# Expert passes: the pass with one expert of 128 rows moves from eighth to tenth, and the weight loads of the last five passes follow

## The chip, the core and the metric

One NeuronCore of one Trainium2 chip runs the whole program. The metric is the device time in microseconds of one execution. Before the change the median of three runs is 1499.13 us (1495.96 to 1499.97). TensorE (PE) does the matrix products, VectorE (DVE) and ScalarE (ACT) the work between them, GpSimd (POOL) issues indexed transfers, and SyncE (SP) issues the weight loads and writes the result.

## The reference, cut to what matters

The program is a two-layer encoder trunk over 512 tokens of width 1024, in float32. Each layer has an attention mixer, which the change leaves alone, and then a grouped top-2 mixture of 16 SwiGLU experts with hidden width 512:

```python
def expert_block(args):
    xb, e = args
    return (jax.nn.silu(xb @ w1[e]) * (xb @ w3[e])) @ w2[e]
...
return jnp.zeros((T, D), h.dtype).at[tok_sorted].add(ys[dest] * g_sorted[:, None].astype(h.dtype))
```

Every token goes to two experts. Each expert has three weight matrices, w1 and w3 (1024 x 512) and w2 (512 x 1024), of 2048 KB each: 48 matrices and 96 MB for each layer.

## The kernel before, in words

**Passes and places.** The experts of a layer are worked off in 11 passes of 128 token rows (`PASSES`). A place is a position in the order in which experts are worked off; `EXPERT_RANK` (line 59) says which expert stands at which place: two experts are fixed (places 0 and 1), the others are sorted on the chip by how many tokens they got, and a place takes the expert of a given rank. `TILES` (line 60) splits each pass into tiles `(place, first row, rows)` of 32, 64 or 128 rows, so that up to four tiles of up to three experts share a pass. Tokens beyond the rows given to a rank go to extra passes behind, under a condition.

**One pass on TensorE** (lines 2405 to 2438, in the order of issue): the first up product (w1, `up_tiles` with m = 0, L2387), the second up product (w3, m = 1, L2387), the transposes of the next pass's tokens (L2353), the down product of the pass before (w2, `down_tiles`, L2398), the transposes of this pass's hidden rows (L2373). So the down product of pass p is issued in pass p + 1. The last pass is different: the down product of pass 9 stands between its two up products, and its own comes last. Ahead of an up product TensorE waits until the weights of all places in that pass have landed (`loaded(j, m)`), ahead of a down product likewise (L2394). When a product is done it adds to a semaphore: `h1_r`, `h3_r` (once for each pass) and `y_r` (twice for each pass).

**Weight slots.** There are eight slots of 2048 KB: six in `ring`, slot 6 is the tile `hT`, slot 7 is `reg_a`. `MOE_LOADS` (line 86) is the list of all 48 loads of a layer as `(place, matrix, slot)`, matrix 0, 1, 2 being w1, w3, w2. A slot is used again for the next load in the list that names it.

**The order of the loads.** It is written out by hand in SyncE's program (lines 706 to 805): a wait for the product that frees the slot, then the load, in the order of `MOE_LOADS`. All of them go to one queue. SyncE is in order, so a load whose slot is free still stands behind the waits of those before it. After the 48 loads come the first weights of the next layer's input projection (`load_z`, layer 0 only), then the read-back of the expert outputs from memory (`load_outputs`, L808).

**Beside them.** GpSimd gathers the token rows of each pass by an indexed transfer from `xn_d` (L916) and scatters the outputs to `ys_d` (L924), each 512 KB, on another queue of the same transfer engines. ScalarE computes the sigmoid and moves transposed data out of PSUM, VectorE multiplies (L1797, L1802) and scales the outputs (L1811).

The lines that the change touches and the prediction's steps use: `EXPERT_RANK` and `TILES` (59 to 70), `MOE_LOADS` (86 to 93), SyncE's loads from place 10 on (757 to 805), TensorE's waits in `loaded` (2376 to 2379) and the loop over passes (2405 to 2441). Passes are numbered from 0 here: the eighth is pass 7, the tenth pass 9.

Of the kernel before, what the change touches and what calls it, by code (L numbers as in the profile page):

```python
# [55 lines left out]

PASSES = 11
STATIC = (11, 12)
EXPERT_RANK = (14, 15, 9, 0, 4, 5, 10, 1, 8, 13, 2, 6, 7, 11, 12, 3)
TILES = (((0, 0, 32), (0, 32, 32), (0, 64, 32), (1, 96, 32)),  # L60
         ((1, 0, 64), (2, 64, 64)),
         ((3, 0, 128),),
# [1 line left out]
         ((5, 0, 64), (6, 64, 64)),  # L64
         ((7, 0, 128),),
         ((8, 0, 32), (8, 32, 32), (8, 64, 32), (9, 96, 32)),
         ((10, 0, 128),),
         ((11, 0, 32), (11, 32, 32), (11, 64, 32), (12, 96, 32)),
         ((12, 0, 32), (12, 32, 32), (13, 64, 32), (14, 96, 32)),
         ((15, 0, 128),))  # L70
FIRST_ROWS = sum(n for j, at, n in TILES[0] if j == 0)

# [1 line left out]
def rows_by_rank():  # L74

    first, rows = [None] * E, [0] * E
    for p, tiles in enumerate(TILES):
        for j, at, n in tiles:
            r = EXPERT_RANK[j]
            first[r] = p * P + at if first[r] is None else first[r]  # L80
# [13 lines left out]
MOE_SLOT = {(j, m): s for j, m, s in MOE_LOADS}  # L94

TR_N1, TR_QK, TR_LAT, TR_KR, TR_N2, TR_X0 = 0, 8, 13, 18, 21, 29
# [88 lines left out]
def trunk(nc, x_in, c_in, w_ada, b_ada, norm1, w_in, q_norm_a, k_norm_a, q_a_norm, kv_norm, w_q_b,  # L185
# [29 lines left out]
    with ExitStack() as ctx:  # L215
# [3 lines left out]
        def sem(name):  # L219
            return ctx.enter_context(nc.semaphore(name))  # L220
# [159 lines left out]
        def slot(s, a, n):  # L380
            if s == R:
                return hT[:, :, :].rearrange("p c n -> p (c n)")[:, 0:a * n].rearrange("p (a n) -> p a n", a=a)
            if s == R + 1:
                return reg_a[:, 0:a * n].rearrange("p (a n) -> p a n", a=a)
            return ring[:, s, 0:a * n].rearrange("p (a n) -> p a n", a=a)
# [125 lines left out]
        h1_r, h3_r = sem("h1_ready"), sem("h3_ready")  # L511
        sge_s = sem("h1_sigmoid")
        u_s_s = sem("expert_hidden")
        y_r, y_e = sem("expert_out_ready"), sem("expert_out_read")
# [33 lines left out]
        def wait(eng, s, value):  # L548

            eng.wait_ge(s, value)  # L550
            eng.sem_inc(ticks, 1)
# [23 lines left out]
        def _(sp):  # L575
# [27 lines left out]
            def load_z(layer, i):  # L603
                at, n = Z_ITEMS[i]
                load(i, (NC, n), in_v[layer, :, :, at:at + n])
# [4 lines left out]
            for l in range(DEPTH):  # L610
# [63 lines left out]
                def load_w1(j, e):  # L674
                    s = MOE_SLOT[j, 0]
                    sp.dma_start(slot(s, NC, F), w1_v[l * E + e]).then_inc(w_rdy[s], 16)

                def load_w3(j, e):
                    s = MOE_SLOT[j, 1]
                    sp.dma_start(slot(s, NC, F), w3_v[l * E + e]).then_inc(w_rdy[s], 16)  # L680

                def load_w2(j, e):
                    s = MOE_SLOT[j, 2]
                    sp.dma_start(slot(s, 4, D), w2_v[l * E + e]).then_inc(w_rdy[s], 16)
# [14 lines left out]
                def expert_at(j):  # L699

                    r = EXPERT_RANK[j]
                    return sp.value_load(order_i[0:1, r:r + 1], min_val=0, max_val=E - 1)
                rank = [None] * E
# [53 lines left out]
                rank[10] = expert_at(10)  # L757
                wait(sp, h3_r, l * PASSES + 6)
                load_w1(10, rank[10])
                wait(sp, y_r, (l * PASSES + 5) * 2)  # L760
                load_w3(10, rank[10])
                wait(sp, y_r, (l * PASSES + 5) * 2)
                load_w2(8, rank[8])
                wait(sp, h1_r, l * PASSES + 7)
                load_w2(9, rank[9])
                rank[11] = expert_at(11)
                wait(sp, h1_r, l * PASSES + 7)
                load_w1(11, rank[11])
                rank[12] = expert_at(12)
                wait(sp, h3_r, l * PASSES + 7)  # L770
                load_w1(12, rank[12])
                wait(sp, h3_r, l * PASSES + 7)
                load_w3(11, rank[11])
                wait(sp, y_r, (l * PASSES + 6) * 2)
                load_w3(12, rank[12])
                wait(sp, h1_r, l * PASSES + 8)
                load_w2(10, rank[10])
                rank[13] = expert_at(13)
                wait(sp, h3_r, l * PASSES + 8)
                load_w1(13, rank[13])  # L780
                rank[14] = expert_at(14)
                wait(sp, y_r, (l * PASSES + 7) * 2)
                load_w1(14, rank[14])
                wait(sp, y_r, (l * PASSES + 7) * 2)
                load_w3(13, rank[13])
                wait(sp, h1_r, l * PASSES + 9)
                load_w3(14, rank[14])
                wait(sp, h3_r, l * PASSES + 9)
                load_w2(11, rank[11])
                wait(sp, y_r, (l * PASSES + 8) * 2)  # L790
                load_w2(12, rank[12])
                rank[15] = expert_at(15)
                wait(sp, h1_r, l * PASSES + 10)
                load_w1(15, rank[15])
                wait(sp, h1_r, l * PASSES + 10)
                load_w2(13, rank[13])
                wait(sp, h1_r, l * PASSES + 10)
                load_w2(14, rank[14])
                wait(sp, h3_r, l * PASSES + 10)
                load_w3(15, rank[15])  # L800
                wait(sp, h3_r, l * PASSES + 10)
                load_w2(15, rank[15])
                if l < DEPTH - 1:
                    wait(sp, h3_r, l * PASSES + 10)
                    load_z(l + 1, 0)

                def load_outputs(t, done):
# [1679 lines left out]
```

## Time and profile before

| what | value |
|---|---|
| median of the runs | 1499.13 us (1495.96 to 1499.97) |
| the profiled execution's own time | 1496.24 us |
| its span, first to last instruction | 1494.5 us |
| PE busy | 1417.9 us (95%) |
| DVE, ACT, POOL busy | 666.3, 397.4, 73.5 us |
| moved by transfers | 346.77 MB, mean 232 GB/s |
| weight loads of the experts | 72 into `ring`, 12 into `reg_a`, 12 into `hT`, 2048 KB each |
| granted TensorE clock, mean | 0.987 |

The busy share of a span is a mean over stages. The expert stages lie at about 490 to 750 us (layer 0) and 1220 to 1475 us (layer 1). An idle time in a timeline row stands in brackets with what ended it. For a transfer the profile gives the instruction that issues it, and the time from there to its landing.

### The profile page before, as it was taken

What the parts mean: (1) busy time and instruction counts of PE and PEld (TensorE: products, weight loads), DVE (VectorE), ACT (ScalarE), POOL (GpSimd) and SP (SyncE); (2) the same over time, 40 slices, a digit from 0 to 9 for tenths busy, and PEclk for the clock granted to TensorE, in tenths of its full rate; (3) what the DMA queues carried; (4) which work ended last, traced back from release to release, by engine and by line L of the source; (5) the groups of instructions that cost most, each with busy time, mean ns of one, the idle gap of its engine ahead of it and who ended that gap; (6) DMA issues with size and microseconds to landing.
All of it is one profiled execution on the core that took longest, in us unless ns stands there. A gap on an engine that the chain in (4) does not pass through costs nothing.

```text
span 1494.5 us, 19619 instructions
## 1 busy us (share of the span) xinstructions
PE 1417.9 (95%) x7656; PEld 790.2 (53%) x7657; DVE 666.3 (45%) x1368; ACT 397.4 (27%) x934; POOL 73.5 (5%) x104
## 2 busy tenths in 40 slices
PE   4989999999998899999999999999999969999997
PEld 2655666777744343343346675677775423343333
DVE  6588676575734311111166877553332260111115
ACT  3227555100012222122041575430001122111212
POOL 1000000000000100100010000000000000011000
PEclk9999999999999899999999999999999979999999
DMA  9963026234273799999976603310306268999994
GB/s 324 383 213 103 18 97 226 85 90 136 94 286 141 294 417 395 422 422 423 368 277 269 173 1 114 114 43 1 113 0 267 94 260 355 412 401 422 425 413 189
DMA packets 113359, 346.77 MB, mean 232 GB/s; under 512 B 26582, under 2 KB 57414, under 8 KB 99888
## 3 DMA queue, kind: packets, MB, share of 16 engines
q1 hardware_dynamic: 87616, 305.68, 53.5%
q0 software_dynamic: 9008, 31.41, 5.6%
q10 hardware_dynamic: 16640, 8.39, 1.9%
q8 instruction: 62, 1.02, 0.3%
q14 instruction: 33, 0.27, 0.1%
HBM read 331.55 MB, written 21.00 MB: 236 GB/s over the span
## 4 chain that ended last, share of the span: by engine, by line
PE 86%; DMA 6%; DVE 4%; ACT 2%; issue 1%; DVEq 1%; SPq 0%; POOLq 0%; ACTq 0%
PE bank L2387 18%; PE bank L2086 13%; PE bank L2398 9%; PE bank L2293 7%; PE bank L2133 7%; PE bank L2016 6%; PE bank L2172 4%; DMA ring<-in_w 3%; PE bank L2228 2%; PE bank L2192 2%; PE bank L2242 2%; PE bank L2201 2%; PE bank L1976 2%; PE bank L1947 2%; DMA ring<-in_w_ada 1%; PE bank L2069 1%
## 5 line engine op out<-in xcount | busy, mean ns | idle before, releaser
L2387 PE MATMUL bank<-ring,reg_b 128*32 128x512 f32 (+2 forms) x1312 | 268.3, 603 | 2.1 <-ACT reg_b L1197 2.1
L2387 PEld LDWEIGHTS bank<-ring,reg_b 128*32 128x32 f32 (+2 forms) x1312 | 86.2, 125 | 139.2 <-issue 136.4
L2398 PE MATMUL bank<-ring,reg_b 128*32 128x512 f32 (+2 forms) x768 | 141.5, 594 | 6.4 <-DMA ring<-in_w 5.0
L2016 PE MATMUL bank<-ring,hT 128*128 128x256 f32 (+3 forms) x448 | 128.6, 448 | 1.2 <-ACT reg_b L1044 1.2
L2293 PE MATMUL bank<-ring,reg_b 128*128 128x512 f32 x256 | 113.0, 596 | 0.0
L2133 PE MATMUL bank<-reg_a,ring 128*128 128x512 f32 x256 | 112.7, 593 | 0.0
L1197 ACT ACTIVATE reg_b<-bank,cur 128x128 f32<-128x128 f32 x176 | 64.0, 470 | 164.7 <-PE bank L2353 164.7
L2016 PEld LDWEIGHTS bank<-ring,hT 128*128 128x128 f32 x448 | 84.8, 190 | 43.1 <-issue 16.5
L1811 DVE TENSOR_TENSOR reg_d<-bank,reg_c 128x512 f32<-128x512 f32 x44 | 30.3, 691 | 135.3 <-PE bank L2398 135.2
L2398 PEld LDWEIGHTS bank<-ring,reg_b 128*32 128x32 f32 (+2 forms) x768 | 47.6, 123 | 78.3 <-issue 75.8
L2086 PE MATMUL bank<-hT,ring 128*128 128x256 f32 x384 | 88.1, 379 | 0.0
L1482 DVE TENSOR_REDUCE nmax<-bank 128x1 f32<-128x512 f32 x128 | 79.5, 684 | 16.1 <-PE bank L2233 12.2
L1797 DVE TENSOR_TENSOR reg_b<-bank,reg_b 128x512 f32<-128x512 f32 x22 | 15.2, 692 | 158.1 <-ACT reg_b L1204 158.1
L2387 PE MATMUL bank<-hT,reg_b 128*32 128x512 f32 (+2 forms) x288 | 84.6, 593 | 0.0
L2086 PEld LDWEIGHTS bank<-hT,ring 128*128 128x128 f32 x384 | 72.8, 190 | 15.8 <-issue 6.7
L2293 PEld LDWEIGHTS bank<-ring,reg_b 128*128 128x128 f32 x256 | 47.7, 190 | 56.3 <-issue 56.3
L2133 PEld LDWEIGHTS bank<-reg_a,ring 128*128 128x128 f32 x256 | 48.5, 190 | 54.6 <-issue 53.9
L1802 DVE TENSOR_TENSOR reg_b<-bank,reg_b 128x512 f32<-128x512 f32 x22 | 15.2, 692 | 123.6 <-PE bank L2387 123.6
L2086 PE MATMUL bank<-ring 128*128 128x256 f32 x256 | 57.9, 379 | 0.0
L2387 PE MATMUL bank<-reg_a,reg_b 128*32 128x512 f32 (+2 forms) x192 | 56.5, 594 | 0.0
L2086 PEld LDWEIGHTS bank<-ring 128*128 128x128 f32 x256 | 48.5, 190 | 6.5
L1204 ACT ACTIVATE reg_b<-bank 128x512 f32<-128x512 f32 x22 | 13.1, 597 | 142.7 <-PE bank L2387 142.7
(352 smaller groups left out, 1951.4 us busy)
## 6 DMA issues: line engine op xcount, KB each, us to landing
ring<-in_w SPq DMA_DIRECT2D x72, 2048.0 KB, 15.4
ring<-in_w_ada SPq DMA_DIRECT2D x16, 2048.0 KB, 11.8
reg_a<-in_w SPq DMA_DIRECT2D x12, 2048.0 KB, 12.8
hT<-in_w SPq DMA_DIRECT2D x12, 2048.0 KB, 15.5
ring<-in_w_in SPq DMA_DIRECT2D x9, 2048.0 KB, 8.0
ring<-in_w_ada SPq DMA_DIRECT2D x16, 512.0 KB, 9.6
vb<-in_w_ada ACTq DMA_DIRECT2D x16, 512.0 KB, 4.0
ring<-in_w_o SPq DMA_DIRECT2D x4, 2048.0 KB, 9.1
```

What stands on the lines that cost most here:

```text
L1197: ins = A(xsT[:, b, cc, :], bank[(p0 + k) % 2][:, c * P:(c + 1) * P], ACT.Identity, scale=scale2(cc), bias=shift2(cc))
L1482: v.tensor_reduce(nmax[:, i:i + 1], bank[4 + i][:, :], X, ALU.max, negate=True).then_inc(mx_s, 1)
L1811: TT(ysb[:, p, cols], bank[6 + n][:, :], g2_row[:, cols], ALU.mult).then_inc(y_e, 1)
L1947: ins = pe.transpose(bank[g % 2][0:rows, t * P:(t + 1) * P], src, ident)
L1976: ins = pe.matmul(bank[z_bank(t)][:, 0:n], hT[:, c, t * P:(t + 1) * P], slot(0, NC, n)[:, c, :], start=c == 0, stop=c == NC - 1)
L2016: ins = pe.matmul(bank[z_bank(k)][:, 0:n], hT[:, c, t * P:(t + 1) * P], w[:, c, :], start=c == 0, stop=c == NC - 1)
L2086: ins = pe.matmul(bank[bk][:, half * 256:(half + 1) * 256], w[:, c, :], tokens[:, c, :], start=c == 0, stop=c == 3)
L2133: ins = pe.matmul(branch_bank(j, q)[:, :], w[:, c, (j % 4) * P:(j % 4 + 1) * P], oT[:, c + 4 * q, :], start=c == 0, stop=c == 3)
L2172: ins = pe.transpose(bank[prob_bank(u)][:, kc * P:(kc + 1) * P], prob[(k - 1) % 2][i][:, kc * P:(kc + 1) * P], ident)
L2293: ins = pe.matmul(wo_bank(k)[:, :], mT[:, c, t * P:(t + 1) * P], w[:, c, :], start=c == 0, stop=c == NC - 1)
L2387: ins = pe.matmul(bank[bk][at:at + n, :], xsT[:, p % 2, c, at:at + n], slot(MOE_SLOT[j, m], NC, F)[:, c, :], start=c == 0, stop=c == NC - 1)
L2398: ins = pe.matmul(bank[6 + h][at:at + n, :], uT[:, c, at:at + n], slot(MOE_SLOT[j, 2], 4, D)[:, c, h * 512:(h + 1) * 512], start=c == 0, s ...
```

## The change

Places 10 to 14 take other ranks: the rank 2 (128 rows) goes from place 10 to place 14, the ranks 6, 7, 11 and 12 each move one place forward. The tiles of passes 7 to 9 follow: pass 7 now has three tiles of place 10 and one of place 11, pass 8 two tiles of place 11, one of place 12 and one of place 13, pass 9 one tile of 128 rows of place 14. Pass 10 is as before. The last 20 of the 48 loads stand in a new order, with slots and waits to match, and the next layer's first `load_z` waits for another product.

```diff
--- before.py
+++ after.py
@@ -56,7 +56,7 @@
 
 PASSES = 11
 STATIC = (11, 12)
-EXPERT_RANK = (14, 15, 9, 0, 4, 5, 10, 1, 8, 13, 2, 6, 7, 11, 12, 3)
+EXPERT_RANK = (14, 15, 9, 0, 4, 5, 10, 1, 8, 13, 6, 7, 11, 12, 2, 3)
 TILES = (((0, 0, 32), (0, 32, 32), (0, 64, 32), (1, 96, 32)),
          ((1, 0, 64), (2, 64, 64)),
          ((3, 0, 128),),
@@ -64,9 +64,9 @@
          ((5, 0, 64), (6, 64, 64)),
          ((7, 0, 128),),
          ((8, 0, 32), (8, 32, 32), (8, 64, 32), (9, 96, 32)),
-         ((10, 0, 128),),
-         ((11, 0, 32), (11, 32, 32), (11, 64, 32), (12, 96, 32)),
-         ((12, 0, 32), (12, 32, 32), (13, 64, 32), (14, 96, 32)),
+         ((10, 0, 32), (10, 32, 32), (10, 64, 32), (11, 96, 32)),
+         ((11, 0, 32), (11, 32, 32), (12, 64, 32), (13, 96, 32)),
+         ((14, 0, 128),),
          ((15, 0, 128),))
 FIRST_ROWS = sum(n for j, at, n in TILES[0] if j == 0)
 
@@ -87,10 +87,10 @@
              (2, 0, 7), (2, 1, 6), (3, 0, 3), (3, 1, 4), (2, 2, 1), (4, 0, 7),
              (5, 0, 5), (4, 1, 6), (5, 1, 0), (3, 2, 3), (6, 0, 4), (6, 1, 2),
              (4, 2, 1), (5, 2, 7), (7, 0, 6), (7, 1, 3), (6, 2, 5), (8, 0, 4),
-             (9, 0, 0), (8, 1, 2), (9, 1, 1), (7, 2, 6), (10, 0, 3), (10, 1, 7),
-             (8, 2, 5), (9, 2, 4), (11, 0, 0), (12, 0, 2), (11, 1, 1), (12, 1, 6),
-             (10, 2, 3), (13, 0, 7), (14, 0, 5), (13, 1, 4), (14, 1, 0), (11, 2, 1),
-             (12, 2, 3), (15, 0, 2), (13, 2, 7), (14, 2, 5), (15, 1, 6), (15, 2, 4))
+             (9, 0, 0), (8, 1, 2), (9, 1, 1), (7, 2, 6), (10, 0, 3), (11, 0, 5),
+             (10, 1, 7), (11, 1, 0), (8, 2, 4), (9, 2, 1), (12, 0, 2), (13, 0, 6),
+             (12, 1, 3), (13, 1, 7), (10, 2, 1), (11, 2, 4), (14, 0, 5), (14, 1, 2),
+             (12, 2, 6), (13, 2, 0), (15, 0, 3), (14, 2, 7), (15, 1, 1), (15, 2, 5))
 MOE_SLOT = {(j, m): s for j, m, s in MOE_LOADS}
 
 TR_N1, TR_QK, TR_LAT, TR_KR, TR_N2, TR_X0 = 0, 8, 13, 18, 21, 29
@@ -757,51 +757,51 @@
                 rank[10] = expert_at(10)
                 wait(sp, h3_r, l * PASSES + 6)
                 load_w1(10, rank[10])
+                rank[11] = expert_at(11)
+                wait(sp, y_r, (l * PASSES + 5) * 2)
+                load_w1(11, rank[11])
                 wait(sp, y_r, (l * PASSES + 5) * 2)
                 load_w3(10, rank[10])
-                wait(sp, y_r, (l * PASSES + 5) * 2)
+                wait(sp, h1_r, l * PASSES + 7)
+                load_w3(11, rank[11])
+                wait(sp, h1_r, l * PASSES + 7)
                 load_w2(8, rank[8])
-                wait(sp, h1_r, l * PASSES + 7)
+                wait(sp, h3_r, l * PASSES + 7)
                 load_w2(9, rank[9])
-                rank[11] = expert_at(11)
-                wait(sp, h1_r, l * PASSES + 7)
-                load_w1(11, rank[11])
                 rank[12] = expert_at(12)
                 wait(sp, h3_r, l * PASSES + 7)
                 load_w1(12, rank[12])
-                wait(sp, h3_r, l * PASSES + 7)
-                load_w3(11, rank[11])
+                rank[13] = expert_at(13)
                 wait(sp, y_r, (l * PASSES + 6) * 2)
+                load_w1(13, rank[13])
+                wait(sp, h1_r, l * PASSES + 8)
                 load_w3(12, rank[12])
-                wait(sp, h1_r, l * PASSES + 8)
+                wait(sp, h3_r, l * PASSES + 8)
+                load_w3(13, rank[13])
+                wait(sp, y_r, (l * PASSES + 7) * 2)
                 load_w2(10, rank[10])
-                rank[13] = expert_at(13)
-                wait(sp, h3_r, l * PASSES + 8)
-                load_w1(13, rank[13])
+                wait(sp, y_r, (l * PASSES + 7) * 2)
+                load_w2(11, rank[11])
                 rank[14] = expert_at(14)
-                wait(sp, y_r, (l * PASSES + 7) * 2)
+                wait(sp, h1_r, l * PASSES + 9)
                 load_w1(14, rank[14])
-                wait(sp, y_r, (l * PASSES + 7) * 2)
-                load_w3(13, rank[13])
                 wait(sp, h1_r, l * PASSES + 9)
                 load_w3(14, rank[14])
+                wait(sp, h1_r, l * PASSES + 9)
+                load_w2(12, rank[12])
                 wait(sp, h3_r, l * PASSES + 9)
-                load_w2(11, rank[11])
+                load_w2(13, rank[13])
+                rank[15] = expert_at(15)
+                wait(sp, h3_r, l * PASSES + 9)
+                load_w1(15, rank[15])
+                wait(sp, h3_r, l * PASSES + 9)
+                load_w2(14, rank[14])
                 wait(sp, y_r, (l * PASSES + 8) * 2)
-                load_w2(12, rank[12])
-                rank[15] = expert_at(15)
+                load_w3(15, rank[15])
                 wait(sp, h1_r, l * PASSES + 10)
-                load_w1(15, rank[15])
-                wait(sp, h1_r, l * PASSES + 10)
-                load_w2(13, rank[13])
-                wait(sp, h1_r, l * PASSES + 10)
-                load_w2(14, rank[14])
-                wait(sp, h3_r, l * PASSES + 10)
-                load_w3(15, rank[15])
-                wait(sp, h3_r, l * PASSES + 10)
                 load_w2(15, rank[15])
                 if l < DEPTH - 1:
-                    wait(sp, h3_r, l * PASSES + 10)
+                    wait(sp, y_r, (l * PASSES + 9) * 2)
                     load_z(l + 1, 0)
 
                 def load_outputs(t, done):
```

## Rows read from the trace of the kernel before

**Rows 1.** The page, section 4: shares by engine of the chain that ended last.
```profile
PE 86%; DMA 6%; DVE 4%; ACT 2%; issue 1%; DVEq 1%; SPq 0%; POOLq 0%; ACTq 0%
```

**Rows 2.** TensorE's waits, whole span: who <- whom: us in total, times, longest us.
```profile
PE bank L2398 <- DMA ring<-in_w: 5.0, 4, 1.8
```

**Rows 3.** Timeline of PE, layer 0: start us, us, what [idle before <- releaser].
```profile
707.80 7.07 PE L2398 MATMUL bank<-ring,reg_b 128*32 128x512 f32 x64 [1.01 <-DMA ring<-in_w]
...
724.12 0.62 PE L2398 MATMUL bank<-ring,reg_b 128*32 128x512 f32 x2 [1.78 <-DMA ring<-in_w]
```

**Rows 4.** Timeline of PE, layer 1, the same places.
```profile
1434.82 1.49 PE L2398 MATMUL bank<-ring,reg_b 128*32 128x512 f32 x12 [1.04 <-DMA ring<-in_w]
...
1450.53 0.62 PE L2398 MATMUL bank<-ring,reg_b 128*32 128x512 f32 x2 [1.18 <-DMA ring<-in_w]
```

**Rows 5.** Table by stretch: length, busy by engine, clock, DMA share, GB/s.
```profile
600.00:700.00 100.00, 100.00 (x604) 39.31 (x600) 12.23 (x18) 17.61 (x42) 9.07 (x9) 1.00 1.01 422
```

**Rows 6.** Timeline of SP, layer 0: start us and length of three issues.
```profile
647.09 0.33 SPq L680 DMA_DIRECT2D hT<-in_w  x1
...
661.34 0.34 SPq L676 DMA_DIRECT2D reg_a<-in_w  x1
...
669.77 0.33 SPq L680 DMA_DIRECT2D ring<-in_w  x1
```

**Rows 7.** Transfers issued by them, in turn: KB, us from issue to landing.
```profile
hT<-in_w SPq DMA_DIRECT2D x1, 2048.0 KB, 23.3
...
reg_a<-in_w SPq DMA_DIRECT2D x1, 2048.0 KB, 19.8
...
ring<-in_w SPq DMA_DIRECT2D x1, 2048.0 KB, 22.2
```

**Rows 8.** The chain of waits in order of time, layer 0: start us, us, what.
```profile
661.98 7.00 PE bank L2398 x64
...
669.57 13.87 PE bank L2387 x128
...
684.53 6.87 PE bank L2398 x16
```

**Rows 9.** Transfers, layer 0, issued at 639.23 us (first row) and 699.11 (second).
```profile
ring<-in_w SPq DMA_DIRECT2D x1, 2048.0 KB, 20.2
...
ring<-in_w SPq DMA_DIRECT2D x1, 2048.0 KB, 13.5
```

**Rows 10.** Timeline of SP, layer 1: two issues.
```profile
1388.33 0.33 SPq L676 DMA_DIRECT2D reg_a<-in_w  x1
...
1396.75 0.33 SPq L680 DMA_DIRECT2D ring<-in_w  x1
```

**Rows 11.** The transfers issued by these two, in turn.
```profile
reg_a<-in_w SPq DMA_DIRECT2D x1, 2048.0 KB, 19.2
...
ring<-in_w SPq DMA_DIRECT2D x1, 2048.0 KB, 21.9
```

**Rows 12.** The chain of waits, layer 1.
```profile
1396.55 13.87 PE bank L2387 x128
...
1411.51 6.87 PE bank L2398 x16
```

**Rows 13.** Timeline of PE, the end of layer 0.
```profile
749.39 1.12 PE L1928 MATMUL bank<-reg_d 128*128 128x512 f32 x2 [1.87 <-DVE reg_d L1811]
```

**Rows 14.** Timeline of PE: two longer waits, and the first up product of layer 1.
```profile
112.40 1.09 PE L1947 MATMUL bank<-cst,reg_b 128*128 128x128 f32 x8 [3.06 <-DVE reg_b L1329]
...
1207.45 0.31 PE L2329 MATMUL bank<-reg_f,cst 128*128 128x64 bf16 x4 [4.11 <-DVE reg_f L1654]
...
1220.56 15.53 PE L2387 MATMUL bank<-ring,reg_b 128*32 128x512 f32 x128 [0.39 <-ACT reg_b L1197]
```

**Rows 15.** Table by stretch, for the clock (the column before the last two).
```profile
100.00:125.00 25.00, 20.38 (x106) 12.85 (x105) 21.11 (x49) 12.02 (x32) 2.98 (x7) 1.00 0.78 211
...
1207.00:1220.00 13.00, 3.94 (x46) 3.48 (x46) 10.48 (x48) 1.00 (x3) 1.08 (x1) 0.50 0.42 136
```

## The prediction

> **What bounds the kernel now.** I read the chain of waits first: PE carries 86% of it and transfers 6% [rows 1]. The change touches only the last part of the two expert stages, so next I read TensorE's waits over the whole execution. Four waits for a weight transfer, all at the down product (L2398), come to 5.0 us [rows 2]. The timeline puts them in the last passes: 1.01 us before the down product of pass 8 and 1.78 us before that of pass 9 in layer 0 [rows 3], 1.04 and 1.18 us at the same places in layer 1 [rows 4]. The stretch table says what they hang on: from 600 to 700 us PE is busy for 100.00 of 100.00 us, the DMA engines stand at a share of 1.01 and move 422 GB/s [rows 5]. So two things are full at once, and the transfers have a backlog: the load issued at 661.34 us takes 19.8 us to land [rows 6, 7], though 2048 KB at 422 GB/s are 5.0 us of work. It stands in line behind some three others.
>
> That gives the model for what follows. All weights go out on SP's queue in the order of the SyncE program, and a weight lands when everything ahead of it has been moved. An earlier issue doesn't bring a landing forward; only an earlier position does.
>
> **The change part by part.**
> *TensorE's work.* Passes 7 to 10 hold the same tiles in another order, and the rows of capacity by rank stay the same, so no expert gets more or fewer rows. Passes of four tiles take 13.87 us for both up products, as the one shown here [rows 8]; the down products of four tiles and of one take 7.00 and 6.87 us [rows 8]. Cost: 0.
>
> *SyncE's work.* 20 weight loads before and after, 20 issues of 0.3 to 0.4 us [rows 6], hidden behind a backlog of about 20 us. If that cover were gone, a late issue would cost at most one place in line, 5 us. The next layer's first z load goes out 21st in line as before, at the down product of pass 8. Cost: 0.
>
> *What each pass asks of the line.* Count loads from w1 of place 10, the first in the changed part, as number 1. Before, the up products of pass 8 need places 11 and 12, and the last of their four weights is number 8. After, they need 11, 12 and 13: w1 of 13 is number 8, needed when the pass starts, and w3 of 13 is number 10, needed at its half. The down product of pass 7 needed number 9 (w2 of 10); after, it needs w2 of 10 and of 11, and the latter is number 12. In return the down product of pass 8 needs number 16 (before: 15), and that of pass 9 number 18 as before, and PE comes to both later by what it has lost.
>
> Now the clock, in layer 0. Number 8 lands at 647.09 + 23.3 = 670.39 us, number 10 at 661.34 + 19.8 = 681.14, number 12 at 669.77 + 22.2 = 691.97 [rows 6, 7]: 10.8 us between each two, 5.4 for one place. I take these landings over to the new order position by position: up to number 12 each position is released by the same event as before, all weights are 2048 KB, and the gathers and scatters beside them keep their times until PE first stalls.
> - Pass 8 starts at 669.57 [rows 8] and waits for number 8: 0.8 us. Its first half (half of 13.87, 6.9) ends at 677.3.
> - The second half waits for number 10 until 681.1: 3.8 us. It ends at 688.1, the token transposes (684.53 - 669.57 - 13.87 = 1.1) at 689.2.
> - The down product of pass 7 waits for number 12 until 692.0: 2.8 us. Before, it began at 684.53 [rows 8]. From here PE is 691.97 - 684.53 = 7.4 us late.
> - Pass 9 would start at about 699.3 and needs numbers 13 and 14; at 5.4 us a place they land at 697.4 and 702.8, the second for its half at 706.2. No wait.
> - The down product of pass 8 would start at 707.80 - 1.01 + 7.4 = 714.2 and needs number 16, which lands at 699.11 + 13.5 = 712.6 [rows 9]: a margin of 1.6 us. The 1.01 us there is gone. Number 18 landed when the wait before pass 9's down product ended, 724.1 [rows 3]; it is now wanted at 724.12 - 1.78 - 1.01 + 7.4 = 728.7. The 1.78 us is gone too.
> - Sum for layer 0: 7.4 - 1.0 - 1.8 = **+4.6 us**.
>
> Layer 1, the same way: number 10 lands at 1388.33 + 19.2 = 1407.53 [rows 10, 11], where the half of pass 8 was due at 1396.55 + 6.9 = 1403.5 [rows 12]: 4.1 us for pass 8. Number 12 lands at 1396.75 + 21.9 = 1418.65 [rows 10, 11], and the down product of pass 7 began at 1411.51 [rows 12]: PE is 7.1 us late, 3.1 of it here. Less 1.04 and 1.18: **+4.9 us**.
>
> What could be given back behind it: at the end of layer 0 PE waits 1.87 us for VectorE's output step [rows 13], which follows outputs read back beside z's load. PE will be later and that load not, so up to 1.87 us of it may go; in layer 1 there is no such wait. I take 0 (PE's own last product sets this end nearly as late) and leave the other end to the range. Bounds of the main term: a whole place in line more or less at number 12 would be +5.4 or -5.4 us in each layer. The row nearest is its own, and over the two layers it stands 7.4 and 7.1 us behind the product that will need it, so I use 1 us each way.
>
> Earlier passes aren't hit: the nearest is the down product of pass 6, which starts at 661.98 [rows 8] and needs number 6, at 639.23 + 20.2 = 659.4 [rows 9]. A margin of 2.5 us.
>
> The sum is +9.5 us on the profiled execution's own 1496.24 us (span 1494.5): 1505.7. The median shown is 1499.13 us, 2.9 above that execution: 1508.6. I forecast between the two, **1507.5 us**.
>
> A rule of the Trainium skill (DMA: Bandwidth & Descriptors, "Queues, rings and completion order") speaks against landings pinned to their position: completion isn't in issue order for one issuing engine. By it number 12 could come a place sooner, 5.4 us, and the sum would be near nothing, about 1498 us. The loads read here land in the order of their issue [rows 6, 7, 9 to 11], so the trace does not bear it out.
>
> **The rivals.**
> *The clock falls in the new waits.* Waits of 3.8 us in the middle of dense work are longer than any that the expert passes have now. For it: behind a wait of 4.11 us in layer 1 the granted clock stood at 0.50 (1.2 GHz) from 1207 to 1220 us [rows 14, 15]. Against: a wait of 3.06 us at 112 us lies in a stretch at 1.00 [rows 14, 15], and at the place of that fall PE had little work for longer than the one wait. Price: that up product took 15.53 us [rows 14] where 13.87 is usual, so 1.7 us for each time. The wait for number 12 hides what follows number 10; one or two falls in each layer that do show are 3.4 to 6.8 us: about 1512. The Trainium skill (TensorE: Matmul & The Clock Gate, "Why this matters for your kernels") says that idle gaps between bursts of matmuls put the clock back to its lower level; by that rule this rival would be the forecast.
>
> *Arrivals keep pace in part.* If releases and not bytes spaced the landings, the earlier places would land earlier. For it: before the change many loads wait for a slot. Against: the share of 1.01 all through [rows 5]. If number 12 landed 4.7 us sooner, nothing is lost or won: about 1498.
>
> *Faster: the waits vanish and nothing comes for them.* One mechanism: a line that isn't full at pass 8, so that number 12 lands before 684.5, 7.4 us earlier than its row. It turns faster from the point where number 12 lands before 687.3. In the end the 5.0 us of [rows 2] are gone: 1499.13 - 5.0 = 1494.1. Against it stands the same share of 1.01.
>
> *Worse: a margin breaks.* The 1.6 us at the down product of pass 8 or the 2.5 us at that of pass 6 fails, and one more place is waited for, 5.4 less the margin, 3 to 4 us in each layer: about 1515.
>
> **How the numbers follow.** Forecast 0.72 (own range 1503.5 to 1511), clock 0.12, in part 0.08, faster 0.04, worse 0.04. 0.3% is 4.5 us, about what a measurement of this kernel can tell from no change: 1494.6 to 1503.6. Faster is the one rival, 0.04; within are "in part" and the low end of the forecast, 0.12; slower 0.84. The range 1502.5 to 1513.5 leaves out faster, "in part", "worse" and the end of the clock's.
>
> **What will show it.** In the changed profile: waits for a weight transfer at L2387 in pass 8, 0.8 and then 3.8 us in layer 0 (4.1 together in layer 1), then 2.8 and 3.1 us at the down product of pass 7; no wait for a transfer at those of passes 8 and 9; numbers 8, 10 and 12 landing within 1 us of the rows here; pass 9 starting 7 us later than before, the last down product 4 to 5 us. If number 10 lands by 677, the model of the line is wrong. If the clock of the stretch behind the waits is under 1.00, the first rival holds.

## The result, and the profile after

The changed kernel takes 1511.1 us (median of 4, 1509.65 to 1513.19) against 1499.55 us for the kernel before, measured beside it (median of 4): ratio 1.0076, 95% interval 1.0063 to 1.0089. Its profiled execution took 1510.24 us (span 1508.5), 14.0 more than that of before. "Late" below is later than before; places in line are counted from w1 of place 10 as number 1, as in the prediction.

TensorE's waits of the kernel after, whole span; these three stand where [rows 2] stood:

```profile
PE bank L2387 <- DMA reg_a<-in_w: 6.7, 2, 3.5
...
PE bank L2398 <- DMA ring<-in_w: 3.5, 2, 1.8
...
PE bank L2387 <- DMA hT<-in_w: 1.7, 2, 1.4
```

5.0 us of waits for weights went and 11.9 us came, partly at another product: L2387 is the up product. The timeline of PE after, layer 0, then layer 1, gives the places; it answers to [rows 3, 4]:

```profile
674.29 0.63 PE L2387 MATMUL bank<-ring,reg_b 128*32 128x512 f32 x3 [0.32 <-DMA hT<-in_w]
...
684.59 0.63 PE L2387 MATMUL bank<-ring,reg_b 128*32 128x512 f32 x3 [3.23 <-DMA reg_a<-in_w]
...
696.22 1.07 PE L2398 MATMUL bank<-ring,reg_b 128*32 128x512 f32 x8 [1.76 <-DMA ring<-in_w]
...
1406.20 0.63 PE L2387 MATMUL bank<-ring,reg_b 128*32 128x512 f32 x3 [1.42 <-DMA hT<-in_w]
...
1416.76 1.07 PE L2387 MATMUL bank<-ring,reg_b 128*32 128x512 f32 x3 [3.48 <-DMA reg_a<-in_w]
...
1428.10 1.49 PE L2398 MATMUL bank<-ring,reg_b 128*32 128x512 f32 x11 [1.71 <-DMA ring<-in_w]
```

They are the start of pass 8 (number 8), its half (number 10) and the down product of pass 7 (number 12). The chain of waits after, layer 0, shows that behind them no weight is waited for: the products of passes 8 to 10 follow each other.

```profile
666.38 7.05 PE bank L2398 x64
...
696.22 7.08 PE bank L2398 x64
...
703.88 13.73 PE bank L2387 x32
...
718.50 7.00 PE bank L2398 x64
...
732.96 6.87 PE bank L2398 x16
```

The loads: SP's timeline (start, length), layer 0, for numbers 8, 10 and 12, and then how long each of the three took to land. They answer to [rows 6, 7]:

```profile
651.22 0.35 SPq L676 DMA_DIRECT2D hT<-in_w  x1
...
665.48 0.33 SPq L680 DMA_DIRECT2D reg_a<-in_w  x1
...
673.57 0.94 SPq L684 DMA_DIRECT2D ring<-in_w  x2
```
```profile
hT<-in_w SPq DMA_DIRECT2D x1, 2048.0 KB, 22.9
...
reg_a<-in_w SPq DMA_DIRECT2D x1, 2048.0 KB, 19.0
...
ring<-in_w SPq DMA_DIRECT2D x1, 2048.0 KB, 22.0
```

Number 12 is the second of the two issues in the third row of SP's timeline, at 674.12. The three land at 674.12, 684.48 and 696.12 us. Pass 5's up product begins at 606.76 (602.71 before), so that is 67.4, 77.7 and 89.4 us behind it; in the trace of before the same positions landed 67.7, 78.4 and 89.3 us behind it. The line is the same in layer 0; what PE asks of it has changed. In layer 1 (pass 5 at 1337.58, before 1329.69) the landings come 68.5, 79.0 and 90.4 us behind, against 67.3, 77.8 and 89.0: 1.2 to 1.4 us later. No run here says why; the other profiles of the changed kernel spread as much there (number 10 ends its wait 76.8 us behind pass 5's start in again, 79.2 in after).

The stretch table after, its columns as in [rows 5]:

```profile
600.00:674.00 74.00, 73.97 (x500) 27.61 (x492) 9.54 (x14) 14.10 (x36) 6.06 (x6) 1.00 1.01 422
...
684.00:694.00 10.00, 9.41 (x70) 3.54 (x71) 0.58 (x1) 0.00 (x0) 0.00 (x0) 0.83 1.04 420
694.00:704.00 10.00, 8.23 (x74) 3.35 (x73) 1.45 (x3) 2.98 (x9) 0.00 (x0) 1.00 0.99 418
...
1416.00:1426.00 10.00, 9.24 (x70) 3.16 (x71) 0.63 (x1) 0.01 (x1) 0.00 (x0) 0.83 1.04 423
```

The transfers run at 1.01 and 422 GB/s as before. New is 0.83 in the clock column (1.00 is 2.4 GHz), just behind the wait for number 10: the second half of pass 8 took 8.77 us instead of 7.07 in layer 0, 8.54 in layer 1. It cost nothing, since number 12 landed later still.

**Where the 14 us are.** I take the distance from the start of pass 5's up product to the start of the last down product as the length of a stage. Before: 137.67 and 137.11 us (layer 0, layer 1); after: 142.06 and 143.13, so +4.4 and +6.0. At the end of layer 0 the wait of [rows 13] is 1.18 us instead of 1.87, 0.7 less. The change need not have done this: in a second profile of the kernel before (experiment before2) it is 1.19 us too. The remaining 4.05 us were there before pass 5 of layer 0 began, ahead of anything that the change touches. The table shows them at about 112 and 515 us:

```profile
112.00:120.00 8.00, 6.89 (x32) 3.23 (x32) 5.21 (x15) 2.05 (x4) 1.31 (x4) 0.57 1.01 328
...
514.00:520.00 6.00, 5.33 (x20) 1.80 (x20) 0.00 (x0) 1.54 (x5) 0.41 (x1) 0.72 0.89 371
```

The clock fell there, and did not in the first trace of before: at 112 us it has 1.00 [rows 15], and at 515 us

```profile
514.00:520.00 6.00, 6.00 (x30) 2.01 (x28) 0.00 (x0) 0.12 (x1) 0.00 (x0) 1.00 0.54 227
```

The second profile of before has both falls too (its table shows 0.76 from 513 to 520 us), at 112 us

```profile
112.00:120.00 8.00, 6.86 (x32) 3.21 (x32) 5.15 (x15) 2.17 (x4) 1.23 (x4) 0.57 1.00 327
```

Its pass 5 begins at 606.65 us, and its span is 1499.3: so this part is chance between executions. Against that span the change costs 9.2 us.

### The profile page after: what moved, and what is told of

It reads as the page before. It is cut to its first block, busy times and chain, and to the rows that moved or that the text cites. A ratio compares the mean times of both kernels' runs of the same rounds, so it can differ in the third digit from the quotient of the medians.

```text
span 1508.5 us, 19619 instructions
## 1 busy us (share of the span) xinstructions
PE 1425.6 (95%) x7656; PEld 794.4 (53%) x7657; DVE 666.2 (44%) x1368; ACT 397.0 (26%) x934; POOL 73.5 (5%) x104
## 4 chain that ended last, share of the span: by engine, by line
PE 86%; DMA 6%; DVE 4%; ACT 2%; issue 1%; DVEq 1%; SPq 0%; POOLq 0%; ACTq 0%
PE bank L2387 18%; PE bank L2086 13%; PE bank L2398 10%; PE bank L2293 7%; PE bank L2133 7%; PE bank L2016 6%; PE bank L2172 4%; DMA ring<-in_w 3%; PE bank L2228 2%; PE bank L2242 2%; PE bank L2201 2%; PE bank L1976 2%; PE bank L2192 2%; PE bank L1947 2%; DMA ring<-in_w_ada 2%; PE bank L2069 1%
## 5 line engine op out<-in xcount | busy, mean ns | idle before, releaser
L2387 PE MATMUL bank<-ring,reg_b 128*32 128x512 f32 (+2 forms) x1344 | 300.7, 610 | 10.6 <-DMA reg_a<-in_w 6.7
L2387 PEld LDWEIGHTS bank<-ring,reg_b 128*32 128x32 f32 (+2 forms) x1344 | 100.3, 130 | 165.4 <-issue 160.9
L2398 PE MATMUL bank<-ring,reg_b 128*32 128x512 f32 (+2 forms) x736 | 127.4, 594 | 4.8 <-DMA ring<-in_w 3.5
L2398 PEld LDWEIGHTS bank<-ring,reg_b 128*32 128x32 f32 (+2 forms) x736 | 40.9, 120 | 69.4 <-issue 62.8
L2387 PE MATMUL bank<-reg_a,reg_b 128*32 128x512 f32 (+1 forms) x256 | 61.4, 614 | 0.0
L2387 PE MATMUL bank<-hT,reg_b 128*32 128x512 f32 (+2 forms) x192 | 56.3, 593 | 0.0
```

The costliest lines, as they stand in the source:

```text
L2387: ins = pe.matmul(bank[bk][at:at + n, :], xsT[:, p % 2, c, at:at + n], slot(MOE_SLOT[j, m], NC, F)[:, c, :], start=c == 0, stop=c == NC - 1)
L2398: ins = pe.matmul(bank[6 + h][at:at + n, :], uT[:, c, at:at + n], slot(MOE_SLOT[j, 2], 4, D)[:, c, h * 512:(h + 1) * 512], start=c == 0, s ...
```

## The experiments

The theory: landings follow from the position in line, and three of the moved passes now ask for positions earlier than before. The rivals: a late issue, waits spread over the whole line, and the clock.

**1. again**, the changed kernel once more.

> The changed kernel once more, unchanged. Theory A (the line of loads: a weight lands when everything ahead of it has been moved, and the change puts the weights of pass 8 and the down product of pass 7 further back): waits for transfers in pass 8 and before the down product of pass 7 come back within 0.5 us (3.2 and 1.8 us in layer 0, 1.4, 3.5 and 1.7 in layer 1), the expert stages together are 9 to 11 us longer than before. The first profile of the changed kernel was 4 us late before it reached the changed part, where the granted clock had fallen twice more than in the profile of before. If that is chance from one execution to the next, it is absent or of another size here and the median is 9.5 to 12 us above before; if the change causes it, it is here again at the same two places.

1508.49 us, 8.8 above before, ratio 1.006 [1.0046, 1.0074]. Of the three places two wait, those of number 10 and number 12; number 8 comes just in time in both layers. The waits did not come back within the 0.5 us expected (3.63 us for 1.76 at the second), and the time is a little under the expected 9.5. The falls at 112 and 515 us are absent. And here the clock held at the wait for number 10 and fell at the next, PE's timeline:

```profile
680.06 0.63 PE L2387 MATMUL bank<-ring,reg_b 128*32 128x512 f32 x3 [2.67 <-DMA reg_a<-in_w]
...
691.86 8.74 PE L2398 MATMUL bank<-ring,reg_b 128*32 128x512 f32 x64 [3.63 <-DMA ring<-in_w]
```

and the stretch just behind it (0.51 in the clock column is 1.2 GHz, with PE busy for all of it):

```profile
691.90:695.30 3.40, 3.40 (x20) 0.90 (x24) 0.00 (x0) 0.00 (x0) 0.00 (x0) 0.51 0.97 414
```

The down product took 8.74 us instead of 7.08, in layer 1 8.77. So the fall can come at either wait. At the first, it eats into the second wait (1.76 instead of 3.63), and at the second it shows. The stages are nearly the same, 142.9 in each layer against 142.1 and 143.1, because the wait for number 12 also ended sooner here, by 0.8 us in layer 0 and 1.9 in layer 1 against pass 5's start.

**2. late10**: issue number 10 later, in the same place in line.

```diff
-                wait(sp, h3_r, l * PASSES + 8)
+                wait(sp, y_r, (l * PASSES + 6) * 2 + 1)
                 load_w3(13, rank[13])
```

> The changed kernel, with one wait moved: load number 10 (w3 of place 13) is issued after the first half of the down product of pass 6, some 3.6 us later than now; its place in the line stays. Theory A: its landing does not move (within 0.5 us, relative to the start of pass 5), the waits in pass 8 stay at 3 to 3.5 us, and the time is that of the changed kernel within 1 us. Rival (a landing follows from its own issue, 19 us later): it lands 3.6 us later, the wait at the half of pass 8 grows to about 7 us, and the time by 1 to 3 us in each layer.

SP's timeline, of again, then of late10, there with PE's row for the half of pass 8:

```profile
661.89 0.33 SPq L680 DMA_DIRECT2D reg_a<-in_w  x1
```
```profile
668.12 0.33 SPq L680 DMA_DIRECT2D reg_a<-in_w  x1
...
681.50 1.07 PE L2387 MATMUL bank<-ring,reg_b 128*32 128x512 f32 x3 [2.54 <-DMA reg_a<-in_w]
```

The issue moved 4.7 us (58.7 to 63.4 us behind pass 5's start). The half of pass 8, which that load releases, begins 76.75 us behind it against 76.88 in again. In layer 1 it begins 1.2 us later than in again (78.05 for 76.84), more than the 0.5 expected; but there the line was late before the moved load: number 7 landed 62.6 us behind pass 5's start (again 61.7). The trace has no landing of number 10 itself, so the end of PE's wait stands for it. The time is 1509.04 us, ratio 1.0058 [1.0044, 1.0072], the same. The moment of issue did not count here, where the line was full.

**3. cut11**: of w2 of place 10 only the first of its four quarters is loaded, so number 11 is 512 KB and everything behind it should land about 4 us sooner.

```diff
-                    sp.dma_start(slot(s, 4, D), w2_v[...]).then_inc(w_rdy[s], 16)
+                    n = 1 if j == 10 else 4
+                    sp.dma_start(slot(s, 4, D)[:, 0:n, :], w2_v[...][:, 0:n, :]).then_inc(w_rdy[s], 16)
```

> The changed kernel, but of w2 of place 10 (load number 11) only a quarter is loaded, so one product uses old data; the issues and waits are the same. Theory A: number 10 lands as before, number 12 lands 3.8 us sooner, the wait before the down product of pass 7 (1.8 and 1.7 us) is gone, and the time is 3.5 us below the changed kernel, not more, since the fall of the clock behind the wait for number 10 (1.7 us in each layer) is no longer hidden by the wait for number 12. Without that fall being on the path it would be 5.7 to 6 us. Rival (releases set the landings): the landings and the time stay.

1500.5 us, ratio 1.0007 [0.9995, 1.0019]. Of the waits for weights this is left (its lines are one higher):

```profile
PE bank L2388 <- DMA reg_a<-in_w: 5.7, 2, 3.2
```

The wait for number 12 is gone in both layers, the one for number 10 has stayed. Number 11 lands 79.9 us behind pass 5's start in layer 0 (again 83.4), and number 14, of full size, 94.9 (98.4): bytes ahead in line set the landing. It brought 8.0 us against again, where 3.5 was expected. In again the second wait is 3.6 us in each layer with a visible fall of 1.7 behind it. The waits went in both layers; the fall went only in layer 1, where none came. In layer 0 it came behind the first wait and now shows (8.77 us). Stages 139.86 and 137.38.

**4. swap**: the kernel before, with only w3 of place 12 moved back from number 8 to number 10. Order of passes, tiles and ranks stay.

```diff
-             ... (11, 1, 1), (12, 1, 6), (10, 2, 3), (13, 0, 7), (14, 0, 5), ...
+             ... (11, 1, 1), (10, 2, 3), (13, 0, 7), (12, 1, 6), (14, 0, 5), ...
-                wait(sp, y_r, (l * PASSES + 6) * 2)
-                load_w3(12, rank[12])
                 ...
                 load_w1(13, rank[13])
+                wait(sp, h3_r, l * PASSES + 8)
+                load_w3(12, rank[12])
```

> The kernel before with its passes as they were, and one load two places later in the line: w3 of place 12 (number 8) becomes number 10, behind w2 of place 10 and w1 of place 13. Theory A: it lands at about 681 us in layer 0, 4.6 us after the half of pass 8 (4.0 in layer 1); the two old waits before the down products of passes 8 and 9 (2.8 and 2.2 us) vanish in exchange. With the clock as it is: +1.8 us in each layer, +3.6 in all over before. If the clock falls in that wait, nothing hides it here: 1.7 us more in each layer, +7 in all. If the loss of the change came from the order of the passes and not from the places in the line, this kernel costs nothing.

1504.66 us, ratio 1.0036 [1.0022, 1.0049]. PE's timeline, layer 0 and 1:

```profile
682.21 0.63 PE L2387 MATMUL bank<-ring,reg_b 128*32 128x512 f32 x3 [3.63 <-DMA hT<-in_w]
...
1414.47 1.07 PE L2387 MATMUL bank<-ring,reg_b 128*32 128x512 f32 x3 [6.17 <-DMA hT<-in_w]
```

The half of pass 8 now needs number 10, and waits as it does in the changed kernel, though no pass was moved; the waits of [rows 3, 4] are gone. The 6.17 us of layer 1 are 2.2 more than expected; why number 10 landed so late there, 79.9 us behind pass 5's start, stays open. The halves behind took 8.77 and 8.43 us, with nothing later to hide them. With both falls 7 us over before were expected: the stages of this profile are 7.3 over the mean of before's (140.26 and 142.47), the median is 5.0 over.

**5. before2**: the kernel before, unchanged, with a profile of its own.

> The kernel before once more, for a second profile of it. Theory A: waits of 1 to 2 us before the down products of passes 8 and 9 in both layers, 4.5 to 6 us in all, no wait for a transfer in pass 8, and the distance from the start of pass 5 to the last down product within 1 us of that of the first profile (137.7 and 137.1 us). The clock falls of the changed kernel behind its waits for weights are absent; falls elsewhere (near 112 us, and in the first passes of layer 1) may come or not, as chance has it, in both kernels.

Ratio 0.9996 [0.9983, 1.0009]. Its waits stand at the same places as [rows 3, 4], 1.60 and 1.81 us in layer 0, 1.08 and 1.78 in layer 1 (the profile puts the 1.08 down to ScalarE); its stages are 138.29 and 137.75 us. So a stage varies by 0.6 us between executions, and the mean of three profiles of the changed kernel (142.6) stands 4.9 us above the mean of two of before (137.7) in each layer: 9.8 us in all.

**6. m_2121**: the one-expert pass from place 8 goes to place 9, not 10, so passes 7 to 10 bring 2, 1, 2, 1 new experts (before 1, 2, 2, 1; after 2, 2, 1, 1). Loads follow.

```diff
-         ((10, 0, 128),),
-         ((11, 0, 32), (11, 32, 32), (11, 64, 32), (12, 96, 32)),
-         ((12, 0, 32), (12, 32, 32), (13, 64, 32), (14, 96, 32)),
+         ((10, 0, 32), (10, 32, 32), (10, 64, 32), (11, 96, 32)),
+         ((12, 0, 128),),
+         ((13, 0, 32), (13, 32, 32), (13, 64, 32), (14, 96, 32)),
          ((15, 0, 128),))
```

> A fourth order: passes 7 to 10 bring 2, 1, 2, 1 new experts, so the pass with one expert of 128 rows is ninth, half the way of the change. Theory A: the last of the four up weights of pass 9 is number 14 in the line; it lands at about 702.5 us in layer 0 and 1429.6 in layer 1, 3.7 us after the half of pass 9 in both, and the two old waits vanish in exchange (2.8 and 2.2 us): +2.5 us over before if the clock stays up, +6 if it falls behind this wait in both layers, since no second wait hides it. Nothing is waited for in pass 8.

1503.32 us, ratio 1.0025 [1.0014, 1.0037]. One place is left that waits, the half of pass 9:

```profile
705.60 8.35 PE L2387 MATMUL bank<-ring,reg_b 128*32 128x512 f32 x64 [3.77 <-DMA ring<-in_w]
...
1434.08 8.77 PE L2387 MATMUL bank<-ring,reg_b 128*32 128x512 f32 x64 [2.37 <-DMA ring<-in_w]
```

The clock fell behind both. This half asks for number 14, where before it asked for number 13. With both falls 6 us over before were expected; 3.5 were measured, as number 14 landed 100.2 us behind pass 5's start in layer 0 but 98.7 in layer 1. So the pass need not go all the way to place 10 to cost: pass 6 brings two new experts as well, and what counts is how many weights PE has asked for by then.

**7. fill and fill2**: the changed kernel with products on constants put in just before the two waits, 5 calls (fill) or 2 (fill2) at each. Nothing reads their result.

```diff
+                def fill(n):
+                    for _ in range(n):
+                        pe.matmul(bank[3][:, :], ident, cst[:, 0:512], start=True, stop=True)
 ...
+                        if p == 8 and m == 1:
+                            fill(2)
 ...
+                        if p == 8:
+                            fill(2)
```

> The changed kernel with ten more products in each layer, which fill its two long waits and feed nothing: five of 128x512 (2.1 us) ahead of the half of pass 8 and five ahead of the down product of pass 7. If the clock falls because TensorE is idle there, it stays at 1.00 in these stretches and the time is 1 to 3.5 us below the changed kernel, whose falls cost 1.7 us each when they come behind the second wait. If the clock has nothing to do with these waits, the time is the same or up to 2 us above, where a wait is shorter than its filling.

> The changed kernel with four more products in each layer that feed nothing, two at each long wait (1.8 us each time; the five of the last such kernel took 4.46 us and outlasted the waits by 1.3 to 2.2 us). They fit into waits of 2.5 us and more. If idle time is what lowers the clock, it stays at 1.00 in passes 8 and 9, and the time is up to 3.4 us below that of the changed kernel in this call (1.7 us for each fall that no later wait hides). If the fall is not on the path, the times are the same.

In fill the 5 calls took 4.56 us,

```profile
679.19 4.56 PE L2393 MATMUL bank<-cst 128*128 128x512 f32 x10
```

outlasted the landings by 1.2 to 2.2 us and so replaced the waits: 1510.56 us, ratio 1.0076 [1.0063, 1.0088]. So it can't give the price of a fall, though the clock stayed at 1.00 in these passes. In fill2 they took 1.9 to 2.0 us and left waits of 1.1 to 1.9:

```profile
681.58 0.63 PE L2387 MATMUL bank<-ring,reg_b 128*32 128x512 f32 x3 [1.11 <-DMA reg_a<-in_w]
...
693.39 7.07 PE L2402 MATMUL bank<-ring,reg_b 128*32 128x512 f32 x64 [1.93 <-DMA ring<-in_w]
```

The table for the ten microseconds behind the first of them, fill2 and then again2:

```profile
682.00:692.00 10.00, 9.46 (x76) 3.77 (x68) 0.69 (x1) 2.66 (x8) 0.00 (x0) 1.00 1.04 419
```
```profile
682.00:692.00 10.00, 9.84 (x72) 3.79 (x72) 0.69 (x1) 0.39 (x2) 0.00 (x0) 0.83 1.05 422
```

**8. again2**, the changed kernel beside fill2 on the same chip.

> The changed kernel, to stand beside the filled one on the same chip: 9 to 11 us above before, waits of some 3 us at the half of pass 8 and 2 to 4 us before the down product of pass 7, the clock down for 3.4 us at one of them in each layer.

1508.36 us, ratio 1.0058 [1.0043, 1.0073]; fill2 1507.89, 1.0055 [1.004, 1.007]. In again2 the clock fell at the first wait in both layers (3.22 us, half product 8.76), and the second wait took it up (1.61). Expected were 9 to 11 us over before; 8.6 were measured. So a clock held at 1.00 in fill2 brought 0.5 us, which can't be told from nothing: where the second wait hides the fall, keeping the clock up is worth nothing that shows.

**9. c_1212**: passes 7 to 10 bring 1, 2, 1, 2 new experts. No two passes with two of them stand together.

```diff
          ((10, 0, 128),),
          ((11, 0, 32), (11, 32, 32), (11, 64, 32), (12, 96, 32)),
-         ((12, 0, 32), (12, 32, 32), (13, 64, 32), (14, 96, 32)),
-         ((15, 0, 128),))
+         ((13, 0, 128),),
+         ((14, 0, 32), (14, 32, 32), (14, 64, 32), (15, 96, 32)))
```

> A third order, made from theory A: passes 7 to 10 bring 1, 2, 1, 2 new experts (before: 1, 2, 2, 1; changed: 2, 2, 1, 1). The pass of place 10 stays eighth, then one expert of 96 rows with one of 32, then one of 128, and the last pass one of 96 with one of 32; the rows for each rank are the same, no expert is shared between these passes, and loads, slots and waits follow. Counting places in the line, every weight lands 3 us or more before it is wanted, except the last w2 (about 1 us). So no wait for a weight is left, the clock does not fall there, and the time is 5.0 us below the kernel before (ratio 0.9967). Rival (any shift of these passes costs, since slots come free later): waits of several us and a time above before.

No wait for a weight is left in either layer: between 600 and 740 us PE has 138.50 of 140.00 us busy. The stages are 134.57 us in both, 6.3 us in all below the mean of before. The time is 1497.16, ratio 0.9984 [0.9973, 0.9995], so only 2.6 us came out, where 5.0 were expected. The end of the layers gave some 4 back: the chain of waits of layer 0 and PE's timeline there:

```profile
730.43 6.76 DMA ys_d<-reg_d,table
...
737.34 6.78 DMA reg_a<-ys_d
```
```profile
748.47 3.70 PE L1928 MATMUL bank<-reg_d 128*128 128x512 f32 x8 [3.39 <-DVE reg_d L1811]
```

The last scatter and the read-back behind it have become the bound there. In layer 0 it is the read-back, beside z's load, that got longer (6.8 us for 5.3 before; the scatter took 6.8 in both), in layer 1 the scatter, beside the last weight loads (6.3 us for 3.5). From the last down product's start to the next product PE now takes 10.46 us (9.01 in before, 8.32 in before2), and from there to the end of layer 1 29.8 (27.7 in both).

**10. c_z**: c_1212, with the next layer's first z load issued behind the first two read-backs of outputs.

> The third order (1, 2, 1, 2 new experts) with one more move: the next layer's first z weights are loaded behind the first two read-backs of outputs instead of ahead of them. In the third order the chain at the end of a layer was no longer PE but the scatter of pass 9 (6.8 us beside other transfers, 3.6 in the kernel before in layer 1) and the read-back (6.8 us). In layer 0 the z load, 5 us of the line, stood ahead of both. Without it the scatter there takes 4 to 5 us and the read-back 5, PE's last down product is the chain again, and 1 to 2 us are gained: 1495 to 1496 us, ratio 0.997. Layer 1 stays as it was. Rival: z lands later than it is wanted and the gain is lost at the first z product.

1494.61 us (1490.25 to 1498.08), ratio 0.9965 [0.9952, 0.9977]: faster than both kernels.

```profile
747.03 3.70 PE L1927 MATMUL bank<-reg_d 128*128 128x512 f32 x8 [1.23 <-DVE reg_d L1810]
```

The wait fell from 3.39 to 1.23 us, and the chain no longer runs over the read-back, which took 4.7 us instead of 6.8; the scatter ahead of it took 6.3 (6.8), not the 4 to 5 expected. What is left is layer 1's end: its scatter takes 6.3 and 6.5 us in these two kernels (c_1212: issued at 1456.43, while the last weight load landed at 1461.96). Before, the last weight landed at 1460.29, one microsecond behind the issue of that scatter, which took 3.5 us; before's transfers, issued from 1459 to 1464:

```profile
ys_d<-reg_d,table POOLq DMA_INDIRECT x1, 3.5
```

In c_1212 PE comes to the scatter sooner, and the loads do not end sooner. No run here tried to part the two.

## Why the prediction was right

The forecast was 1507.5 us in 1502.5 to 1513.5, and slower. Measured: 1511.1, and 1508.5 and 1508.4 in the two repeats. The mechanism was right; that the number held is in part luck, as the point on the sum says.

- **The model of the line.** Right, and shown twice: late10 moved an issue 4.7 us and in layer 0 nothing behind it (in layer 1 the line was late already), cut11 took 1536 KB out ahead of number 12 and its wait went. Landings taken over by position hold within 0.7 us in layer 0, the bound that the prediction set was 1; in layer 1 they came 1.2 to 1.4 us later, beyond it. The Trainium skill (DMA: Bandwidth & Descriptors, "Queues, rings and completion order") doesn't promise completion in the order of issue; in the traces here the 2048 KB loads of this queue did land in that order.
- **Which places wait.** Right: number 8, number 10, number 12, and no others; number 8, whose wait is the shortest, is in time in again. The sizes were 0.8, 3.8 and 2.8 us for layer 0; measured 0.3, 3.2 and 1.8 with the clock's 1.7 between the last two. Pass 8 came up a little later against its loads than read from before. PE stands 7.6 us late at the down product of pass 7 (7.4 predicted): what a wait does not take, the fall does, because number 12 sets the end of both. In layer 1 it is 8.7 for 7.1, nearly all of it number 12's later landing.
- **What goes.** Right: the waits of [rows 3, 4] are gone. The smallest margin, predicted at 1.6 us for number 16, was 1.2 in layer 0 (landed 717.3, wanted 718.4) and held, and no earlier pass was hit. Of SyncE's issues, taken at 0.3 to 0.4 us each, that of number 18 took 8.9 us in both layers, at no cost to the waits.
- **The sum.** +9.5 predicted, +4.6 and +4.9. Measured on the stages +10.4 between the two first profiles, +9.8 between the means. The profile of after also holds the clock falls at 112 and 515 us, some 4 us, which the first profile of before does not; whether they explain its median, 3.6 above the forecast, can't be read from runs without a profile. The two repeats, against 1499.7 us each, cost 8.8 and 8.6 us. Falls of the clock stood at 0 in the sum. In after and again2 the later wait hid the falls; in again both showed, 3.4 us, and the stages stayed near +10 only because number 12's wait ended 0.8 and 1.9 us sooner than in after.
- **The cost that was left at 0.** Rightly: the 0.7 us by which the wait at the end of layer 0 is shorter is there in the second profile of before as well.
- **The rival of the clock.** Its mechanism was given 0.12 and happened in every profile of the changed kernel, once in each layer. Its price was right, 1.7 us a fall (8.77 for 7.07), and so was the sentence that the wait for number 12 hides it. What failed is the comparison with the 3.06 us wait at 112 us, which lay in a stretch at 1.00 [rows 14, 15]: it was one execution's luck, and in before2 and after the clock fell at the same place. In passes 7 to 9 of all runs ten of eleven waits of 3.2 to 3.8 us had one behind them, so it has to be counted as likely; what it costs depends on whether a later wait covers it. The Trainium skill (TensorE: Matmul & The Clock Gate, "Why this matters for your kernels") speaks of idle gaps between bursts that put the clock back, and the traces agree in part: 0.51 behind a wait of 3.63 us in again, but no fall behind one of 3.35 us in layer 1 of late10.
- **The other rivals.** "Arrivals keep pace in part", "faster" and "a margin breaks" are refuted by the landings and by the chain of waits in these profiles. That another order of the same passes could go under the kernel before, without the waits, was in the prediction only as a line that isn't full; c_1212 got there with a full line, by asking for each weight later.

Several expectations of the experiments missed in size. again and again2 came out under the 9.5 and 9 us expected, and their waits were split otherwise. cut11 brought 8.0 us for 3.5, swap and m_2121 cost less than with both falls expected. fill was sized too large to be a test. Most of c_1212's gain in the stage was lost to the scatter and read-back at the end of the layers.

## What to carry to other kernels

Where one queue of loads is always full, as here, take a load's landing from its position: number the loads, take the landing of each number from the trace, and ask of a new order only which number each product waits for and when it comes to it. Put work that needs few new weights between passes that need many, so that the demand never runs ahead of the line. Then look at what stood behind the waits: in c_1212 the shorter stage brought its last scatter and read-back onto the path, and moving one load behind them brought some of it back. Take a second profile of the kernel before as well: here the first lacked two clock falls, some 4 us, that the second had.

## What the runs showed of the hardware

- In passes 7 to 9 the clock fell to 1.2 GHz for about 3.4 us (1.7 us lost each time) behind waits for a weight of 2.4 to 3.8 us, and held behind others of the same size: 2.54 us in late10 brought a fall, while 2.67 us in again, 2.46 us in cut11 and 3.35 us in late10 did not. At the wait of 6.17 us (swap) it fell 2 us into the wait and stayed low for 6.8 us. Behind single waits of up to 2.1 us in these passes it never fell. Early in the stage it did: at 515 us in after and before2, behind waits of 1.24 and 0.67 us on ScalarE, but not in before at the same place. Even the same wait did both (112 us in before and before2). What decides between them stays open.
- 2048 KB loads landed 4.9 to 7.5 us apart in layer 0 of after (numbers 4 to 20), 5.4 in the mean, with gathers and scatters between them, at 418 to 425 GB/s, whatever waits of PE lay beside them.
- The last scatter of layer 1 took 6.3 and 6.5 us beside weight loads (c_1212, c_z), and 3.5 us where the last load landed one microsecond behind its issue (before). Those ahead of it took up to 11 us.
- An issue on SP's queue that otherwise takes 0.33 us took 3.6 us with four loads not yet landed (number 19, before) and 8.9 us with six (number 18, after).
